# The triangular inverse's levels: products in four array quadrants, a head mask crossed over the partition halves, and weight lows on GpSimd

## The chip, the cores and the metric

One core of a Trainium2 chip runs the whole kernel in one launch. The metric is the device time of one execution in microseconds (us). TensorE multiplies matrices into PSUM; VectorE and ScalarE work elementwise on SBUF and PSUM; GpSimd works elementwise on SBUF alone; SyncE issues the DMAs. Each engine runs its own list of instructions in order, and they wait for one another by semaphores.

## The reference

Two blocks follow one another on 512 tokens of width 1024. The first is an attention and convolution block. The second mixes tokens with twelve recurrent heads of width 64 (an RWKV-7 delta rule) and a small cross attention, and ends with a feed-forward layer. What matters here is the recurrence of the second block:

```
def step(S, inp):
    r_t, w_t, k_t, v_t, a_t, b_t = inp
    sa = jnp.einsum('bhvk,bhk->bhv', S, a_t)
    S = (S * w_t[:, :, None, :] + sa[..., None] * b_t[:, :, None, :]
         + v_t[..., None] * k_t[:, :, None, :])
    return S, jnp.einsum('bhvk,bhk->bhv', S, r_t)
```

The inputs r, k, v come from projections of the normed residual with 1024-row weights; w and a come through low-rank products and sigmoids.

## The kernel before, in words

The recurrence is computed in chunks. The 512 tokens are eight chunks of 64, and inside a chunk the steps become products of 64 by 64 matrices, for which a unit lower triangular matrix of each chunk must be inverted. Two heads are worked on together, a pair; there are six pairs, numbered 0 to 5 (`for p in range(NP)`, on TensorE and on VectorE alike). A tile of 128 partitions holds two chunks at a time, the even one in partitions 0 to 63 and the odd one in 64 to 127 (`PARITIES`, index q), four of these double chunks (`G`, index c) and two heads (index h) side by side. `rows(0)` is the first 64 partitions, `rows(1)` the others.

**The inverse.** Its blocks are doubled level by level: `LEVELS` is 2, 4, 8, 16, 32. In each level b, for each head, TensorE multiplies the strict triangle NT with the inverse so far, XN (`times_inverse`, L1310). VectorE masks the result to the level's band and writes it to Y (L2606). TensorE multiplies Y with XT in both orders (`inverse_update`, L1323 and L1326; in the last level only one, L1336). VectorE adds that to XT and XN (L2641). The next level's product waits for head h's add, separately for each head. Operands and results of one such matmul are 64 partitions high, so each uses a quadrant of the 128x128 array. The stationary and moving operands of `times_inverse` lie in the half 1-q, the output in the half q: of the array's four quadrants, this product uses the two crossed ones. A head's product is eight matmuls, each two instructions in fp32.

**What stands between.** The engines' lists are written out by hand. Between a level's products and its updates, and behind the updates, TensorE has other work: the projection of the next pair's values (half of it in level 4 ahead of the update, the other half behind it), a low-rank gate product in level 8, a sum of squares in level 16, `masked_values` (L1349) behind level 8, sums of a norm (L1237, L1238) behind level 2. In levels 2 to 16 VectorE has the decayed keys and norms of other pairs. At level 8 it starts with `pair_input(p + 1, "v")` (L2067), which waits for ScalarE's part (L1841), then masks, then for p < 5 `unit_key` (L2064) and `bonus_rest` (L2481), then the two adds. Behind the levels come `solve`, the transitions and a chain of six states, beside which the projections of the pair after next run.

**Weights in two parts.** A projection is done as three fp32r matmuls per tile: weights high with data high and low, weights low with data high (L857 to L859). ScalarE rounds a 128x1024 block to its high part (`weights_high`, L1673); VectorE subtracts it from the block to get the low part (`weights_low`, L2123) and raises `w_low`. The product waits for `w_high` and `w_low`; the DMA that refills the block's place waits for `w_low`. The blocks stand in the order of `SPLIT`, and `w_low` counts them. For the pairs' blocks VectorE does this where `weights_after` is called, often several us after the high part is there.

**GpSimd** does four fills and, for pairs 0 and 1, the decayed key KD (L809).

Of the kernel before, what the change touches and what calls it, by code (L numbers as in the profile page):

```python
# [40 lines left out]
F32 = mybir.dt.float32  # L41
F32R = mybir.dt.float32r
ALU = mybir.AluOpType
# [18 lines left out]
C = 64  # L62
NC = S // C
# [19 lines left out]
STEPS = NQ * QT  # L83
MTILES = S // P
MUNITS = 2 * MTILES
MU_AMID, MU_BEHIND = {0: 0, 1: 2, 2: 3, 4: 5}, {0: 1, 3: 4}
MU_SOLVE = len(MU_AMID) + len(MU_BEHIND)
MU_CHAIN = MU_SOLVE + 1
# [331 lines left out]
def build(nc, small, tables, xT, ctxT, memT, weights, saved, outT):  # L420
    plan = psum_plan()
    with ExitStack() as ctx:
# [269 lines left out]
        def group(q):  # L692
            return sum(q >= SPLIT_AT[n] for n in ("out0", "wdad", f"mix{PAIR_MIX}"))
# [21 lines left out]
        def free_inc(ins, name):  # L715
            ins.then_inc(free[plan[name][0]], 1)
# [78 lines left out]
        @block.gpsimd  # L795
        def _(pool):
            pool.memset(QW[:], 0.0).then_inc(filler_ready, 1)
            pool.memset(SILU[:], 0.0).then_inc(zeroed, 1)
            pool.wait_ge(*is_full("ctx_sum"))
            pool.memset(GLU, 0.0).then_inc(zeroed, 1)  # L800
            pool.wait_ge(*is_full("h1_sum"))
            pool.memset(H[:, 0, :], 0.0).then_inc(zeroed, 1)

            for p in range(2):

                pool.wait_ge(bonus_in, p + 1)
                pool.wait_ge(exps_done, p + 1)
                k3, l3 = (x.rearrange("p (c t) -> p c t", c=NC) for x in (QW[:], LG))
                pool.tensor_tensor(KD[p % 2], k3, l3, ALU.mult).then_inc(kd_ready, 1)  # L809


        @block.tensor
        def _(pe):
# [481 lines left out]
            def key_products(name, p, x):  # L1295
                take(name)
                out = by_head(name)
                for c in range(G):
                    for q, h in QH:
                        ins = pe.matmul(out[rows(q), h, c], x[rows(h), 2 * c + q, :],  # L1300
                                        AR[p % 2][rows(h), :, 2 * c + q, :], start=True, stop=True)
                        if c == G - 1:
                            full_inc(ins, name)

            def times_inverse(name, h):

                out = take(name, G * C).rearrange("p (c t) -> p c t", c=G)
                for c in range(G):
                    for q in range(PARITIES):
                        ins = pe.matmul(out[rows(q), c, :], NT[rows(1 - q), h, c, :], XN[rows(1 - q), h, c, :],  # L1310
                                        start=True, stop=True)
                        if c == G - 1:
                            full_inc(ins, name)
# [104 lines left out]
            for p in range(NP):  # L1418
# [14 lines left out]
                for b in LEVELS:  # L1433
                    for h in range(HEADS):
                        if prev is None:
                            pe.wait_ge(x_first, p + 1)
                        else:
                            pe.wait_ge(*is_free(f"x{prev}_{p}_{h}"))
                        times_inverse(f"y{b}_{p}_{h}", h)

                    if p == NP - 1:
                        if b == LEVELS[0]:
                            gn_mean(p - 1)
                        if b == LEVELS[1]:
                            gn_square(p - 1)
                        if b == LEVELS[3]:
                            gate_low_rank(p - 1)
                        memory_unit(MU_AMID.get(LEVELS.index(b)))
                        if b == LEVELS[2]:
                            masked_values(p)  # L1450
                    else:
                        if b == LEVELS[1]:
                            project_part(f"v_{p + 1}", 0, DK // 2)
                        if p and b == LEVELS[2]:
                            gate_low_rank(p - 1)
                        if p and b == LEVELS[3]:
                            gn_square(p - 1)
                        if b == LEVELS[-1] and p + 2 < NP:
                            low_rank(p + 2)
                    for h in range(HEADS):  # L1460

                        pe.wait_ge(*is_free(f"y{b}_{p}_{h}"))
                        if b != LEVELS[-1]:
                            inverse_update(f"x{b}_{p}_{h}", h)
                        else:

                            last_update(f"xf_{p}_{h}", h)
                    if p == NP - 1:
                        memory_unit(MU_BEHIND.get(LEVELS.index(b)))
                    else:  # L1470
                        if p and b == LEVELS[0]:
                            gn_mean(p - 1)
                        if b == LEVELS[1]:
                            project_part(f"v_{p + 1}", DK // 2, DK)
                        if b == LEVELS[2]:
                            masked_values(p)
                        if b == LEVELS[3]:
                            bonus_sum(p + 1)
                        if b == LEVELS[-1]:
                            project_part(beside_chain(p, "k"), 0, 2)  # L1480
                    prev = b
# [572 lines left out]
        def _(vec):  # L2054
# [63 lines left out]
            def weights_low(q):  # L2118

                b = BLOCK_AT[SPLIT[q]]  # L2120
                vec.wait_ge(w_high, q + 1)
                high, low = wsplit(q)
                vec.tensor_tensor(low, room_of(b), high.bitcast(F32), ALU.subtract).then_inc(w_low, 1)  # L2123
# [322 lines left out]
                i = "krv".index(x)  # L2446
                free_inc(shift_end(f"{x}_{p}", 3 + 3 * p + i, MU_PAIR + 3 * p + i, (K0, R0, V0)[i]), f"{x}_{p}")

            def weights_after(p, x):

                if group(SPLIT_AT[f"{x}_{p}"] + 2) == 2:
                    weights_low(SPLIT_AT[f"{x}_{p}"] + 2)

            def chunks(x):
                return x.rearrange("p (c t) -> p c t", c=NC)

# [108 lines left out]
            for p in range(2):  # L2565
                denominator(f"w_{p}")
                denominator(f"A_{p}")
                running_sums(p)
                for x in "kr":
                    pair_input(p, x)  # L2570
                    weights_after(p, x)
                changed_key(p)
                least_norm(p)
                if p == 0:
                    pair_input(0, "v")
                    weights_after(0, "v")
                    bonus(0)
                    decayed_r(0)
                    unit_key(0)
                    decayed_a(0)  # L2580
                    scaled_b(0)
                    decayed_b(0)
                else:
                    decayed_r(1)
            for p in range(NP):
# [14 lines left out]
                for b in LEVELS:  # L2600
                    if p + 1 < NP and b == LEVELS[2]:
                        pair_input(p + 1, "v")
                    for h in range(HEADS):
                        name = f"y{b}_{p}_{h}"
                        vec.wait_ge(*is_full(name))
                        free_inc(vec.tensor_tensor(Y[:, h], bank(name, G * C).rearrange("p (c t) -> p c t", c=G),  # L2606
                                                   mask(f"m{b}", G), ALU.mult), name)

                    if p == NP - 1 and b == LEVELS[0]:
                        gn_centre(p - 1)  # L2610
# [30 lines left out]
                        free_inc(vec.tensor_tensor(old, new, old, ALU.add), name)  # L2641
                    if late and b == LEVELS[1]:
                        decayed_r(late)
                        weights_after(late, "r")
                    if norm_late(p - 1):
                        if b == LEVELS[0]:
                            gn_centre(p - 1)
# [14 lines left out]
                    return x.rearrange("p (c q) t -> p q c t", q=PARITIES)  # L2662

                if p + 1 < NP:
                    weights_after(p + 1, "v")
                    if norm_late(p - 1):
                        gn_finish(p - 1)
                        gate(p - 1)
                    if late:
                        decayed_key(late)  # L2670
                else:
                    for m in range(PAIR_MIX):
                        weights_low(SPLIT_AT[f"mix{m}"])
                    memory_unit(MU_SOLVE)
# [10 lines left out]
                for n in CHAIN:  # L2685
                    name = f"h_{p}_{n}"
                    if p == NP - 1 and n in MU_STEPS:
                        memory_unit(MU_CHAIN + n - 1)
                    vec.wait_ge(*is_full(name))
                    free_inc(scaled_sum(H[:, n + 1, :], bank(name, C), ELC[p % 2][:, n:n + 1], FB[:, n, :]), name)  # L2690
                    if p == NP - 2 and n == G:
                        memory_queries(0)
                    if p == NP - 1 and n in MIXED_AT:
                        if n == min(MIXED_AT):
                            vec.wait_ge(*is_full(f"yu_{p}"))
                        for k in MIXED_AT[n]:
                            mixed_low(k)
                    if p + 2 < NP:
                        if n == 1:
                            denominator(f"w_{p + 2}")  # L2700
                        if n == 2:
                            denominator(f"A_{p + 2}")
                        if n == 3:
                            running_sums(p + 2)
                        if n == 4:
                            pair_input(p + 2, "k")
                        if n == 5:
                            weights_after(p + 2, "k")
                            key_squares_rest(p + 2)
                if p + 2 < NP:  # L2710
                    pair_input(p + 2, "r")
# [214 lines left out]
```

## Time and profile before

| | us |
|---|---|
| median of 3 runs (1069.06 to 1071.4) | 1069.5 |
| the profiled execution | 1070.18 |
| its span | 1068.4 |
| TensorE matmul busy | 1039.6 (97%) |
| VectorE busy | 653.9 (61%) |
| ScalarE busy | 453.0 (42%) |
| GpSimd busy | 5.6 (1%) |
| granted TensorE clock, as a share of full speed | 1.0 |

Busy shares are over the whole span. The levels of the six pairs stand between 386 and 653 us. The ends of matmuls are modelled, so neighbours overlap by some 0.07 us in the list; the distance from start to start is what one costs.

### The profile page before, as it was taken

What the parts mean: (1) busy time and instruction counts of PE and PEld (TensorE: products, weight loads), DVE (VectorE), ACT (ScalarE), POOL (GpSimd) and SP (SyncE); (2) the same over time, 40 slices, a digit from 0 to 9 for tenths busy, and PEclk for the clock granted to TensorE, in tenths of its full rate; (3) what the DMA queues carried; (4) which work ended last, traced back from release to release, by engine and by line L of the source; (5) the groups of instructions that cost most, each with busy time, mean ns of one, the idle gap of its engine ahead of it and who ended that gap; (6) DMA issues with size and microseconds to landing.
All of it is one profiled execution on the core that took longest, in us unless ns stands there. A gap on an engine that the chain in (4) does not pass through costs nothing.

```text
span 1068.4 us, 22579 instructions
## 1 busy us (share of the span) xinstructions
PE 1039.6 (97%) x9816; PEld 823.4 (77%) x9816; DVE 653.9 (61%) x1025; ACT 453.0 (42%) x732; POOL 5.6 (1%) x10
## 2 busy tenths in 40 slices
PE   7999999999999989999999999999999999999998
PEld 5777777676777777777777767787888888888887
DVE  4569999977466665868677667664443223444322
ACT  5455555686335533443535245344432112443111
POOL 0000000000000000000000000000000000000000
PEclk9999999999999999999999999999999999999999
DMA  9912224000532110110110121322222232223230
GB/s 360 377 61 99 79 81 176 1 2 2 197 118 79 60 42 22 43 42 25 39 42 22 42 81 43 124 93 99 99 99 99 99 99 88 93 96 114 89 104 30
DMA packets 26161, 95.01 MB, mean 89 GB/s; under 512 B 2896, under 2 KB 3152, under 8 KB 25552
## 3 DMA queue, kind: packets, MB, share of 16 engines
q1 hardware_dynamic: 26064, 93.57, 25.1%
q8 instruction: 79, 1.29, 0.5%
q14 instruction: 18, 0.15, 0.0%
HBM read 89.36 MB, written 4.19 MB: 88 GB/s over the span
## 4 chain that ended last, share of the span: by engine, by line
PE 76%; DVE 16%; ACT 4%; issue 2%; DMA 1%; SPq 1%; POOL 0%; ACTq 0%; DVEq 0%
PE psum L857 19%; PE psum L858 18%; PE psum L859 18%; DVE work L2067 5%; PE psum L867 3%; PE psum L1310 2%; PE psum L1323 2%; DVE small_temps L2218 1%; PE psum L1045 1%; PE psum L1024 1%; PE psum L1359 1%; PE psum L1382 1%; DMA work<-weights 1%; DVE in_weights_low L2123 1%; PE psum L1110 1%
## 5 line engine op out<-in xcount | busy, mean ns | idle before, releaser
L2123 DVE TENSOR_TENSOR weights_low<-ring,weights_high 128x1024 fp32r<-128x1024 f32 x70 | 85.8, 1226 | 75.3 <-ACT weights_high L1673 75.3
L1673 ACT ACTIVATE weights_high<-ring 128x1024 fp32r<-128x1024 f32 x70 | 73.6, 1052 | 127.5 <-PE psum L859 127.5
L857 PE MATMUL psum<-normed_high,weights_high 128*128 128x512 f32 x256 | 100.2, 391 | 0.2 <-DVE weights_low L2123 0.2
L859 PE MATMUL psum<-normed_high,weights_low 128*128 128x512 f32 x256 | 99.7, 389 | 0.0
L859 PE MATMUL psum<-hidden_high,weights_low 128*128 128x512 f32 x256 | 99.7, 389 | 0.0
L858 PE MATMUL psum<-normed_low,weights_high 128*128 128x512 f32 x256 | 99.6, 389 | 0.0
L858 PE MATMUL psum<-hidden_low,weights_high 128*128 128x512 f32 x256 | 99.6, 389 | 0.0
L857 PE MATMUL psum<-hidden_high,weights_high 128*128 128x512 f32 x256 | 99.6, 389 | 0.0
L2067 DVE SCALAR_TENSOR_TENSOR work<-work,small_sb 128x512 f32<-128x512 f32 x116 | 80.2, 745 | 0.2
L1643 ACT ACTIVATE work<-psum 128x384 f32<-128x384 f32 (+1 forms) x110 | 54.1, 541 | 56.3 <-PE psum L1359 18.8
L857 PE MATMUL psum<-pair_normed_high,pair_weights_high 128*128 128x512 f32 x176 | 75.8, 431 | 0.8 <-DVE normed_low L2127 0.8
L858 PE MATMUL psum<-normed_low,pair_weights_high 128*128 128x512 f32 x176 | 69.3, 394 | 0.0
L859 PE MATMUL psum<-pair_normed_high,pair_weights_low 128*128 128x512 f32 x176 | 68.9, 392 | 0.0
L2046 ACT ACTIVATE work<-work 128x512 f32<-128x512 f32 x32 | 20.2, 632 | 100.9 <-DVE work L2064 100.9
L857 PE MATMUL psum<-normed_high,in_weights_high 128*128 128x512 f32 x144 | 59.2, 411 | 1.9 <-DVE in_weights_low L2123 1.6
L857 PEld LDWEIGHTS psum<-normed_high,weights_high 128*128 128x128 f32 x256 | 48.1, 188 | 10.8 <-issue 0.9
L859 PE MATMUL psum<-normed_high,in_weights_low 128*128 128x512 f32 x144 | 56.2, 390 | 0.0
L858 PE MATMUL psum<-normed_low,in_weights_high 128*128 128x512 f32 x144 | 56.2, 390 | 0.0
L859 PEld LDWEIGHTS psum<-normed_high,weights_low 128*128 128x128 f32 x256 | 48.1, 188 | 10.1
L858 PEld LDWEIGHTS psum<-normed_low,weights_high 128*128 128x128 f32 x256 | 48.1, 188 | 10.1 <-issue 0.2
L859 PEld LDWEIGHTS psum<-hidden_high,weights_low 128*128 128x128 f32 x256 | 48.1, 188 | 10.0
L857 PEld LDWEIGHTS psum<-hidden_high,weights_high 128*128 128x128 f32 x256 | 48.1, 188 | 9.9
(320 smaller groups left out, 2102.6 us busy)
## 6 DMA issues: line engine op xcount, KB each, us to landing
ring<-weights SPq DMA_DIRECT2D x135, 512.0 KB, 3.7
work<-weights SPq DMA_DIRECT2D x10, 512.0 KB, 12.9
residual<-xT SPq DMA_DIRECT2D x4, 512.0 KB, 7.1
mixed<-weights SPq DMA_DIRECT2D x4, 512.0 KB, 7.8
residual_saved<-residual SPq DMA_DIRECT2D x8, 256.0 KB, 4.4
residual<-residual_saved SPq DMA_DIRECT2D x1, 2048.0 KB, 9.0
outT<-residual SPq DMA_DIRECT2D x8, 256.0 KB, 3.3
tables_sb<-tables SPq DMA_DIRECT2D x1, 1280.0 KB, 10.4
```

Of the source, the lines that this page charges most:

```text
L857: pe.matmul(out, wh, high(k), start=first and n == 0, stop=False)
L858: pe.matmul(out, wh, low(k), start=False, stop=False)
L859: ins = pe.matmul(out, wl, high(k), start=False, stop=last and n == len(order) - 1)
L867: full_inc(pe.matmul(take(name, w), stationary, moving, start=True, stop=True), name)
L1024: last = pe.transpose(out[:, t * P:(t + 1) * P], src[:, t * P:(t + 1) * P], tab("ident"))
L1310: ins = pe.matmul(out[rows(q), c, :], NT[rows(1 - q), h, c, :], XN[rows(1 - q), h, c, :], start=True, stop=True)
L1323: ins = pe.matmul(out[rows(q), 0, c, :], Y[rows(q), h, c, :], XT[rows(q), h, c, :], start=True, stop=True)
L1643: free_inc(act.activation(out, bank(name, w) if src is None else src, ACT.Copy), name)
L1673: act.activation(wsplit(q)[0], room_of(b), ACT.Copy).then_inc(w_high, 1)
L2046: act.activation(FS[:, t, :], FS[:, t, :], ACT.Square).then_inc(h_relu, 1)
L2067: return vec.scalar_tensor_tensor(out=out, in0=a, scalar=scalar, in1=b, op0=op, op1=ALU.add)
L2123: vec.tensor_tensor(low, room_of(b), high.bitcast(F32), ALU.subtract).then_inc(w_low, 1)
```

## The change

`times_inverse_both` takes the place of `times_inverse` in levels 4, 8, 16 and 32 (`CROSSED`); level 2 keeps the old form. It issues both heads' matmuls interleaved. Head 0's output goes to the half q as before, head 1's to the half `q ^ 1`, the same as its operands' half, so all four quadrants are used in turn. Both heads' tiles are full at the end, and both heads' adds of the level before are waited for at the start. Head 1's result then lies with its halves exchanged, and VectorE masks it in two instructions of 64 partitions, each reading one half and writing the other.

The lows of the 18 blocks from v_0 to qm1 go from VectorE to GpSimd, with KD of pair 0 behind v_0's and KD of pair 1 behind r_1's; `weights_after` is gone.

```diff
+CROSSED = (4, 8, 16, 32)
 ...
-            for p in range(2):
-
-                pool.wait_ge(bonus_in, p + 1)
-                pool.wait_ge(exps_done, p + 1)
-                k3, l3 = (x.rearrange("p (c t) -> p c t", c=NC) for x in (QW[:], LG))
-                pool.tensor_tensor(KD[p % 2], k3, l3, ALU.mult).then_inc(kd_ready, 1)
+            def weights_low(q):
+                b = BLOCK_AT[SPLIT[q]]
+                pool.wait_ge(w_high, q + 1)
+                high, low = wsplit(q)
+                pool.tensor_tensor(low, room_of(b), high.bitcast(F32), ALU.subtract).then_inc(w_low, 1)
+            first = SPLIT_AT["v_0"]
+            pool.wait_ge(w_low, first)
+            for q in range(first, SPLIT_AT["mix0"]):
+                weights_low(q)
+                if SPLIT[q] in ("v_0", "r_1"):
+                    p = 0 if q == first else 1
+                    pool.wait_ge(bonus_in, p + 1)
+                    pool.wait_ge(exps_done, p + 1)
+                    k3, l3 = (x.rearrange("p (c t) -> p c t", c=NC) for x in (QW[:], LG))
+                    pool.tensor_tensor(KD[p], k3, l3, ALU.mult).then_inc(kd_ready, 1)
 ...
+            def times_inverse_both(p, b):
+                names = [f"y{b}_{p}_{h}" for h in range(HEADS)]
+                outs = [take(name, G * C).rearrange("p (c t) -> p c t", c=G) for name in names]
+                for c in range(G):
+                    for q in range(PARITIES):
+                        for h in range(HEADS):
+                            ins = pe.matmul(outs[h][rows(q ^ h), c, :], NT[rows(1 - q), h, c, :],
+                                            XN[rows(1 - q), h, c, :], start=True, stop=True)
+                            if c == G - 1:
+                                full_inc(ins, names[h])
 ...
-                        times_inverse(f"y{b}_{p}_{h}", h)
+                        if b not in CROSSED:
+                            times_inverse(f"y{b}_{p}_{h}", h)
+                    if b in CROSSED:
+                        times_inverse_both(p, b)
 ...
-                        free_inc(vec.tensor_tensor(Y[:, h], bank(name, G * C).rearrange("p (c t) -> p c t", c=G),
-                                                   mask(f"m{b}", G), ALU.mult), name)
+                        y, m = bank(name, G * C).rearrange("p (c t) -> p c t", c=G), mask(f"m{b}", G)
+                        if h == 0 or b not in CROSSED:
+                            ins = vec.tensor_tensor(Y[:, h], y, m, ALU.mult)
+                        else:
+                            for half in range(2):
+                                ins = vec.tensor_tensor(Y[rows(half), h], y[rows(1 - half)], m[rows(1 - half)], ALU.mult)
+                        free_inc(ins, name)
 ...
                 else:
+                    vec.wait_ge(w_low, SPLIT_AT["mix0"])
                     for m in range(PAIR_MIX):
                         weights_low(SPLIT_AT[f"mix{m}"])
```

## Rows read from the trace of the kernel before

**Rows 1.** The page, busy time, share of the span and instructions of each engine

```profile
PE 1039.6 (97%) x9816; PEld 823.4 (77%) x9816; DVE 653.9 (61%) x1025; ACT 453.0 (42%) x732; POOL 5.6 (1%) x10
```

**Rows 2.** VectorE's line L2123 by tile (ns, min/median/max), and waits of TensorE, 386 to 670

```profile
L2123 DVE TENSOR_TENSOR pair_weights_low<-ring,pair_weights_high x24: 1214/1218/1226, 320.0 to 654.3; 128x1024 fp32r<-128x1024 f32 x24
...
PE psum L1323 <- DVE work L2606: 1.5, 4, 0.9
```

**Rows 3.** Groups of TensorE, 480 to 760 us: busy us, mean ns of one

```profile
L1310 PE MATMUL psum<-work 64*64 64x64 f32 x640 | 23.2, 221 | 0.7 <-DVE work L2641 0.5 <-issue 0.2
...
L1382 PE MATMUL psum<-work 64*64 64x64 f32 x512 | 8.3, 219 | 0.0
```

**Rows 4.** Timeline of TensorE: start us, us, instruction, idle before

```profile
389.30 1.15 PE L1310 MATMUL psum<-work 64*64 64x64 f32 x32 [0.16 <-DVE work L2641]
...
485.54 1.15 PE L1310 MATMUL psum<-work 64*64 64x64 f32 x32
...
493.61 1.15 PE L1310 MATMUL psum<-work 64*64 64x64 f32 x32
494.69 0.70 PE L867 MATMUL psum<-work,small_sb 128*128 128x512 f32 x1
...
497.67 1.15 PE L1310 MATMUL psum<-work 64*64 64x64 f32 x32
...
501.17 1.15 PE L1310 MATMUL psum<-work 64*64 64x64 f32 x32
...
503.45 1.15 PE L1336 MATMUL psum<-work 64*64 64x64 f32 x32
504.53 0.50 PE L857 MATMUL psum<-pair_normed_high,pair_weights_high 128*128 128x512 f32 x1
...
598.45 1.15 PE L1336 MATMUL psum<-work 64*64 64x64 f32 x32 [0.42 <-DVE work L2606]
```

**Rows 5.** Timeline of VectorE, pair 0 and pair 2

```profile
388.73 0.96 DVE L2641 TENSOR_TENSOR work<-psum,work 128x256 f32<-128x256 f32 x2 [0.43 <-PE psum L1326]
...
484.53 0.95 DVE L2641 TENSOR_TENSOR work<-psum,work 128x256 f32<-128x256 f32 x2 [0.43 <-PE psum L1326]
...
494.52 0.75 DVE L2067 SCALAR_TENSOR_TENSOR work<-psum,small_sb,work 128x511 f32<-128x511 f32 x1 [1.41 <-ACT work L1841]
495.18 0.74 DVE L2606 TENSOR_TENSOR work<-psum,tables_sb 128x256 f32<-128x256 f32 x2
495.85 0.74 DVE L2064 SCALAR_TENSOR_TENSOR work<-work,small_sb,head_rstd 128x512 f32<-128x512 f32 x1
496.50 0.69 DVE L2481 TENSOR_TENSOR bonus_low<-t_t,bonus_high 128x512 fp32r<-128x512 f32 x1
497.11 0.75 DVE L2641 TENSOR_TENSOR work<-psum,work 128x256 f32<-128x256 f32 x2
...
502.26 0.75 DVE L2606 TENSOR_TENSOR work<-psum,tables_sb 128x256 f32<-128x256 f32 x2
```

**Rows 6.** Timeline of ScalarE, level 8 of pair 2

```profile
494.38 1.05 ACT L1673 ACTIVATE pair_weights_high<-ring 128x1024 fp32r<-128x1024 f32 x1
```

**Rows 7.** Timeline of VectorE, instructions over 64 partitions

```profile
336.65 0.41 DVE L2074 TENSOR_SCALAR sigmoids<-sigmoids 64x512 f32<-64x512 f32 x1
337.10 0.42 DVE L2415 COPY work<-t_t 64x512 f32<-64x512 f32 x1
```

**Rows 8.** Timelines of GpSimd and VectorE around 381 us, and the same copy at 491

```profile
381.61 1.28 POOL L809 TENSOR_TENSOR work<-weighted,work 128x512 f32<-128x512 f32 x1 [21.15 <-DVE t_t L2064]
...
381.44 0.69 DVE L2485 TENSOR_SCALAR head_rstd<-psum 128x512 f32<-128x512 f32 x1
382.05 0.87 DVE L2497 COPY small_temps<-work 128x8 f32<-128x8 f32 x1
...
491.21 0.16 DVE L2497 COPY small_temps<-work 128x8 f32<-128x8 f32 x1
```

**Rows 9.** Timeline of VectorE, head of pair 0

```profile
385.34 1.22 DVE L2593 TENSOR_TENSOR work<-work,tables_sb 128x1024 f32<-128x1024 f32 x1
```

More of the change, by code:

```diff
@@ L2447, in pair_input @@
                 free_inc(shift_end(f"{x}_{p}", 3 + 3 * p + i, MU_PAIR + 3 * p + i, (K0, R0, V0)[i]), f"{x}_{p}")
-            def weights_after(p, x):
-                if group(SPLIT_AT[f"{x}_{p}"] + 2) == 2:
-                    weights_low(SPLIT_AT[f"{x}_{p}"] + 2)
             def chunks(x):
@@ L2570, in _ @@
                     pair_input(p, x)
-                    weights_after(p, x)
                 changed_key(p)
@@ L2575, in _ @@
                     pair_input(0, "v")
-                    weights_after(0, "v")
                     bonus(0)
@@ L2643, in _ @@
                         decayed_r(late)
-                        weights_after(late, "r")
                     if norm_late(p - 1):
@@ L2664, in _ @@
                 if p + 1 < NP:
-                    weights_after(p + 1, "v")
                     if norm_late(p - 1):
@@ L2707, in _ @@
                         if n == 5:
-                            weights_after(p + 2, "k")
                             key_squares_rest(p + 2)
```

## The prediction, made before the result was known

> **What bounds the kernel now.** I read the page's busy shares first. TensorE is busy for 97% of the span [rows 1]: a microsecond of it left empty is a microsecond of time. VectorE and GpSimd are far below that, so moving work between them pays only where TensorE waits for VectorE. The view of who waited for whom, from 386 to 670 us, has as its largest sum 1.5 us, TensorE on the masks [rows 2]. So the 18 weight lows taken off VectorE (1.22 us each [rows 2]) have little to give back, and the extra work has little room.
>
> Then the order of time. The changed code stands in six pairs of heads, some 48 us each, and I followed pair 2 [rows 4, 5]. Below, "+t" counts from the start of the level's product with NT. The reader is to see in rows 4 that TensorE goes from group to group without a hole, and in rows 5 that in level 8 VectorE does so too, from the values' input to the adds.
>
> **The product in four quadrants.** A level's product is 32 instructions (each matmul is two in fp32). In two quadrants the next group comes 1.08 us after its start (493.61 to 494.69, [rows 4]). By the sums, 640 such instructions take 23.2 us, 36 ns each, while 512 of a product that goes round all four quadrants take 8.3 us, 16 ns [rows 3]. At 16 to 18 ns the 32 take 0.6 us. So 0.48 us per level, 24 levels, 11.5 us, is the most this part can return, and only where nothing else comes last.
>
> **What it adds on VectorE.** Head 1's mask becomes two instructions over 64 partitions. Half the partitions is not half the time: a tensor_scalar over 64x512 took 0.41 us and a copy of 64x512 0.42 us [rows 7]. The copy also shows a second cost. It reads and writes the other half of the partitions than its predecessor, has no wait, and starts 0.04 us after that one's end, where neighbours overlap by 0.08 (334 to 339 against 495.18 to 497.77, [rows 5, 7]). The two half masks change halves each, and so does what follows them. So I take 0.46 us from start to start for these three, where masks without a wait are 0.33 apart. What follows comes later by 0.33 us if nothing is held and by 3 x 0.46 - 2 x 0.33 = 0.71 us if all three are; I take the latter, by the row of the copy. The Trainium skill (VectorE: DVE Perf Modes, section on two Vector instructions with no wait between them) says that an instruction whose input or output starts in another quadrant than the last one's is held until the earlier ones have finished. The trace agrees, with the 0.04 us.
>
> It also ties the heads together: a product of levels 4 to 32 now needs both adds of the level before, where head 0's needed only the first, and head 1's update needs the second half mask. Level 2 itself is unchanged.
>
> **Level 4** (between product and update stand 12 matmuls of a projection). Level 2's adds end at 485.48, and the product started at 485.54 anyway [rows 4, 5]. The masks are hidden, and the adds, behind VectorE at 491.21 [rows 8], are needed at 493.61: -0.48 us, all of it. Pair 0 started level 4 on the first add (389.30, while the second ended at 389.69 [rows 4, 5]): +0.44 takes that back.
>
> **Level 8 is where the change meets itself.** VectorE comes here with the values' input at +0.91, which hangs on ScalarE's part and that on the projection, not on the product. Then mask, mask, unit key, bonus low, add, add, without a hole, and level 16 starts at 497.67, +4.06 [rows 4, 5]. The shorter product gains nothing: TensorE would be through the gate product at +1.65, but mask 0 starts at +1.57 and ends at +2.0. The second half mask ends at +2.92, and what follows is 0.71 late; the adds start at +4.2 and +4.55, the second ends at +4.97 and level 16, which now waits for it, starts at +5.0 if nothing else happens: +0.95.
>
> Now GpSimd. ScalarE's weights high ends at 495.43 [rows 6], +1.82. VectorE made the low long after, at a quiet place; GpSimd starts it at once, about +1.9. How long it takes no row shows: its product over 128x512 took 1.28 us [rows 8], so 128x1024 is between 2.3 (if it grows as VectorE's does, from 0.69 to 1.22 us, [rows 2, 5]) and 2.56 us (twice). I take 2.4, up to +4.3. The unit key (L2064), all of whose tensors lie in SBUF, wants to start at +2.95. What happens to such an instruction? The one place where GpSimd and VectorE overlap is 381.61 to 382.89. VectorE's L2485, reading PSUM, ran its usual 0.69 us. The copy L2497, SBUF to SBUF, lasted 0.87 us against 0.16 elsewhere, and ended with GpSimd's instruction [rows 8]. I take it that the unit key is stopped the same way until +4.3. Then 0.65 to the bonus low, 0.61 to the adds, 0.33 and 0.42 for these: +6.3. Level 16 starts at +6.35, so +2.3 us. Masks and adds read one operand from PSUM and run on. The Trainium skill (SBUF — State Buffer, section on the two sides of SBUF) says that VectorE and GpSimd share a port pair as an exclusive lock, for a VectorE instruction in a two-port mode or with two SBUF inputs, and that the loser waits out the whole instruction. It supports the step from copy to two-input product, which the trace does not show.
>
> This holds for the five pairs that have the values' projection at level 8 (pairs 0 to 4). Elsewhere GpSimd's low starts behind ScalarE's high beside instructions that read PSUM, or has 2.8 us of these in front of it: nil.
>
> **Level 16.** One sum stands between product and update. Mask 0 can start at +0.77, the half masks at +1.23 and +1.69, the last ends at +2.12; head 1's update then runs from +2.17 to +2.87, its add ends at +3.5 behind the decayed a, and level 32 starts at +3.56, against +3.50 (497.67, 501.17, [rows 4]). +0.06. Pair 0 has no sum of squares there, its update waited for the mask alone, and by the same chain it loses 0.5.
>
> **Level 32.** A low-rank product stands in between (pairs 0 to 3). After the second add VectorE has two instructions of 0.6 us, then mask 0 at +1.06, halves at +1.52 and +1.98, the last ends at +2.41. TensorE is through at +1.81 (2.28 before, 501.17 to 503.45 [rows 4]) and does head 0's update, 0.54 us; head 1's starts at +2.46, and the next projection at +3.0 instead of +3.36 (504.53, [rows 4]): -0.32. Pair 4 has nothing in between and already waited for its mask, 0.42 us (598.45, [rows 4]); the last half mask comes 0.35 late there: +0.35.
>
> **Sum.** Pairs 1 to 3: -0.48 + 2.3 + 0.06 - 0.32 = 1.56 us, 4.7 in all. Pair 4: 2.2. Pair 0: -0.04 + 2.3 + 0.5 - 0.32 = 2.4. Pair 5 has no GpSimd work; its waits for both adds and longer mask chains against shorter products: +0.2, an estimate. Before the first pair: the first low is on TensorE's way at its start, +0.15. And the pair's head: the lows of v_1 and k_2 (GpSimd's queue holds them behind the second decayed key) now fall on 382 to 387, where VectorE has the copy, L2500, three masks from PSUM and L2593, whose two inputs are both in SBUF and which releases level 2 [rows 8, 9]. VectorE comes there up to 1.2 us earlier without its own low, GpSimd's two times 2.4 us then stop L2500 and L2593 in turn. L2593 starts about 387.5 instead of 385.34: +2.2 (bounds -0.7 and +3.9, if GpSimd loses or wins every contest). Together 4.7 + 2.2 + 2.4 + 0.2 + 0.15 + 2.2 = 11.9 us. The profiled execution took 1070.2 us (span 1068.4), so 1082.1; the median of three was 0.7 less: 1081.
>
> SP's loads wait for the lows. Those of r_1 to r_2 come 1 to 6 us later, at least 3 us ahead of their use; later ones come earlier. Nil.
>
> **Rivals.**
> 1. Only SBUF copies are stopped, not products with two inputs. Then level 8 costs 0.95: pairs 1 to 3 0.2 each, pair 4 0.9, pair 0 1.1, pair 5 0.2, the head -0.7, 0.15. Sum +2.3: 1072. For it: the only stopped instruction seen is a copy.
> 2. GpSimd is slower than twice its 128x512, or wins each contest: 3.4 us instead of 2.4 adds 1 us in five levels, 0.5 at L2593 in the pairs' heads, and takes the 3.9: about +20, 1089. For it: the page calls GpSimd's spans rough.
> 3. The other side, faster: TensorE's product is what counts. Nothing stops the unit key and nothing holds the halves, which start 0.33 apart. Level 4 gives 0.48, level 16 0.3, level 32 0.48; level 8 still costs 0.6 for one mask more and the second add. That is -0.65 in pairs 1 to 3, about +0.1 in pairs 0 and 4 together, -0.3 in pair 5, and -0.7 in the head: -2.9 + 0.15, 1067. It decides if, in level 8, the second add ends by +4.6. Against it: rows 7 and 8. If moreover a half mask cost half, level 8 would be as before and the time 1064.
>
> **Chances.** Forecast 0.63 (own range 1078 to 1085, from 2.3 to 2.56 us for a low and the head's bounds), rival 1 0.18, rival 2 0.06, rival 3 0.13. A measurement tells 0.2%, 2.1 us, from no change: faster 0.1 (most of rival 3), within 0.13 (the rest of it and half of rival 1), slower 0.77. The range 1068 to 1087 takes in rival 1 and leaves out rival 2 and most of rival 3.
>
> **What would show it.** GpSimd with 18 instructions of 128x1024, near 2.4 us (much above 3: rival 2). L2064 in level 8 lasting about 2 us or starting late, and ending with GpSimd's: the stop; 0.75 us beside a running GpSimd: rival 1. Half masks 0.46 apart or 0.33. TensorE without work for some 2 us ahead of level 16's product in five pairs. Level 4's product followed after 0.6 us by the projection; if after 1.08, the four quadrants do not run together and the part gives nothing (+4 us on the sum). The whole argument is wrong if level 16 still starts near +4.1.

## The result, and the profile after

The changed kernel takes 1082.37 us (median of 4 runs, 1081.04 to 1084.09) where the kernel before takes 1069.28 beside it: ratio 1.0115, 95% interval 1.0093 to 1.0138. It is slower, by 13.1 us. The profiled execution took 1084.09 us, span 1082.3, which is 13.9 more than the span before.

The page after, busy time, share of the span and instructions of each engine:

```profile
span 1082.3 us, 22605 instructions
PE 1039.7 (96%) x9816; PEld 818.8 (76%) x9816; DVE 653.0 (60%) x1031; ACT 453.0 (42%) x732; POOL 50.4 (5%) x28
```

Against [rows 1], TensorE did the same number of instructions in the same busy time, and its idle time grew from 28.8 to 42.6 us. The equal busy time is a balance of two things: in the kernel of the first experiment, with the new product and masks alone, it is 1034.3 us, 5.3 less, and the changed kernel spends 13.7 us at the lower clock, where its instructions last longer. GpSimd has 18 instructions more and 45 us. VectorE lost the 18 lows (22 us) and yet is busy for only 0.9 us less. 24 masks became 48 halves of the same length (+10 us, at 0.42 each); the other 11 us are instructions that now last longer.

The waits of TensorE from 386 to 684 us (us in total, times, longest):

```profile
PE psum L1324 <- DVE work L2666: 9.6, 8, 1.5
PE psum L1347 <- DVE work L2628: 3.6, 9, 1.4
PE psum L1347 <- DVE work L2631: 2.4, 9, 0.3
```

L1324 is the product in four quadrants, L2666 the adds of the level before. Before, the largest sum of this view was 1.5 us [rows 2]; now TensorE waits 9.6 us for the adds, 7.6 of them in five waits at the end of level 8. Level 8 is the place. Timelines of pair 1, first TensorE, then VectorE, then GpSimd (start us, us, instruction, idle before):

```profile
449.54 0.69 PE L1324 MATMUL psum<-work 64*64 64x64 f32 x32
450.16 1.13 PE L879 MATMUL psum<-work,small_sb 128*128 128x512 f32 x2
...
455.71 0.69 PE L1324 MATMUL psum<-work 64*64 64x64 f32 x32 [1.52 <-DVE work L2666]
```

```profile
450.45 0.75 DVE L2094 SCALAR_TENSOR_TENSOR work<-psum,small_sb,work 128x511 f32<-128x511 f32 x1 [1.81 <-ACT work L1868]
451.12 0.41 DVE L2628 TENSOR_TENSOR work<-psum,tables_sb 128x256 f32<-128x256 f32 x1
451.56 0.86 DVE L2631 TENSOR_TENSOR work<-psum,tables_sb 64x256 f32<-64x256 f32 x2
452.45 1.89 DVE L2091 SCALAR_TENSOR_TENSOR work<-work,small_sb,head_rstd 128x512 f32<-128x512 f32 x1
454.26 0.68 DVE L2503 TENSOR_TENSOR bonus_low<-t_t,bonus_high 128x512 fp32r<-128x512 f32 x1
454.87 0.74 DVE L2666 TENSOR_TENSOR work<-psum,work 128x256 f32<-128x256 f32 x2
```

```profile
451.44 2.35 POOL L810 TENSOR_TENSOR pair_weights_low<-ring,pair_weights_high 128x1024 fp32r<-128x1024 f32 x1 [14.59 <-ACT pair_weights_high L1700]
```

The product's follower comes 0.62 us after its start (1.08 before, [rows 4]): the quadrants do run together. But the unit key (L2091), 0.74 us in [rows 5], lasts 1.89 us and ends 0.55 us after GpSimd's low (453.79). The adds end behind it, and level 16 starts at +6.17 where it started at +4.06. TensorE stands 1.52 us right before that product, in pairs 0 to 4 alike. The half masks (L2631) run wholly beside the same low; they read one operand from PSUM, write to SBUF, and keep their 0.43 and 0.42 us.

Level by level, start to start, in us (before / after), read from the starts of the level's product:

| pair | level 2 | level 4 | level 8 | level 16 | level 32 to next pair |
|---|---|---|---|---|---|
| 0 | 2.65 / 3.13 | 8.10 / 8.51 | 4.06 / 6.16 | 3.05 / 4.44 | 28.84 / 30.12 |
| 1 | 3.09 / 3.16 | 8.07 / 7.61 | 4.07 / 6.17 | 3.50 / 4.44 | 30.38 / 29.68 |
| 2 | 3.08 / 3.20 | 8.06 / 7.61 | 4.06 / 6.17 | 3.50 / 4.44 | 28.89 / 28.63 |
| 3 | 3.09 / 3.17 | 8.07 / 7.69 | 4.06 / 6.17 | 3.93 / 3.57 | 28.96 / 28.80 |
| 4 | 3.09 / 3.17 | 8.06 / 7.65 | 4.07 / 6.17 | 3.50 / 3.57 | 30.11 / 30.46 |
| 5 | 5.74 / 5.74 | 4.95 / 4.92 | 5.36 / 6.08 | 5.78 / 5.84 | |

The first product of the first pair starts 0.26 us earlier than before (386.40 against 386.66), so nothing was lost up to there.

Level 16 has two lengths, and the reason stands in the granted clock. Stretches of the kernel after (columns: us, then busy us of TensorE, weight loads, VectorE, ScalarE, GpSimd with counts, granted clock, DMA share, GB/s): the first in level 16 of pair 1, the second of pair 2, the third in levels 16 and 32 of pair 0, the last in level 16 of pair 3:

```profile
457.10:460.50 3.40, 3.40 (x78) 2.58 (x82) 2.90 (x7) 1.23 (x2) 0.00 (x0) 0.51 0.02 5
508.30:511.70 3.40, 3.40 (x82) 2.51 (x80) 2.87 (x7) 1.14 (x2) 0.00 (x0) 0.51 0.00 0
405.90:412.70 6.80, 6.58 (x107) 4.03 (x98) 5.08 (x10) 0.89 (x2) 0.00 (x0) 0.50 0.00 0
558.00:561.00 3.00, 2.75 (x100) 2.00 (x98) 2.92 (x8) 1.23 (x2) 0.00 (x0) 1.00 0.03 10
```

The clock is at the lower of its two levels, 1.2 GHz, in three of five pairs, beginning 1.4 to 1.7 us after TensorE resumed work in level 16. In the profiled execution before the change it was at the upper one, 2.4 GHz, all through the recurrences. Pair 3's level 16, 3.93 before the change, holds a stall inside its product (0.23 us, during which TensorE waits for nothing that the profile shows), so its 3.57 is no gain of the change.

### The profile page after: what moved, and what is told of

The parts are those of the page before. It is cut to its first block, busy times and chain, and to the rows that moved or that the text cites. A ratio compares the mean times of both kernels' runs of the same rounds, so it can differ in the third digit from the quotient of the medians.

```text
span 1082.3 us, 22605 instructions
## 1 busy us (share of the span) xinstructions
PE 1039.7 (96%) x9816; PEld 818.8 (76%) x9816; DVE 653.0 (60%) x1031; ACT 453.0 (42%) x732; POOL 50.4 (5%) x28
## 4 chain that ended last, share of the span: by engine, by line
PE 72%; DVE 19%; ACT 4%; issue 2%; DMA 1%; SPq 1%; POOL 0%; ACTq 0%; DVEq 0%
PE psum L869 19%; PE psum L870 18%; PE psum L871 18%; DVE work L2094 6%; PE psum L879 2%; DVE small_temps L2245 2%; DVE work L2091 1%; DMA ring<-weights 1%; PE psum L1347 1%; PE psum L1057 1%; PE psum L1324 1%; PE psum L1036 1%; PE psum L1383 1%; PE psum L1406 1%; DVE work L2631 1%
```

## The experiments

**The two halves of the change apart, and the lows moved or cut.** Four kernels. Products alone: the four-quadrant product and the crossed masks, with the lows on VectorE.

> The change's products and crossed masks alone; all lows on VectorE as before. Theory (GpSimd's product stops VectorE's instructions that have all tensors in SBUF, and holds the unit key of level 8): level 8 takes 5.0 us from its product to level 16's instead of 6.17, level 4 7.6, and the time is 1069.3 + about 3 = 1072. Rival A (the crossed masks and the wait for both adds are the cost, GpSimd's lows nearly free): level 8 still near 6 us, 1080 or more.

Lows alone: GpSimd makes them, products and masks as before.

> GpSimd's lows alone; products and masks as before. Theory: in level 8 the unit key is still stopped, for it could start at +2.24 and GpSimd holds it to about +4.3, so the level takes 5.9 us instead of 4.06, in five pairs, less 0.5 at the first pair's head: 1069.3 + 9 = 1078, more if TensorE's clock falls as it did in the change's profile. Rival A: near 1069.

Lows late: the changed kernel, but the one low that falls on level 8 waits for the pair's last add.

```diff
+            late = {SPLIT_AT["qm1" if p + 2 == NP else f"r_{p + 2}"]: p for p in range(NP - 1)}
             for q in range(first, SPLIT_AT["mix0"]):
+                if q in late:
+                    pool.wait_ge(*is_free(f"xf_{late[q]}_1"))
                 weights_low(q)
```

> The whole change, but the five lows that fell on level 8 (r_2 to r_5 and qm1) wait on GpSimd for the second add of level 32, the place where VectorE made them. Theory: the unit key lasts 0.75 us again, level 8 takes 5.0 us, no granted clock under 1.0 in the pairs, and the time is some 0.5 us under the products-only kernel: 1071.5. Rival A: 1082 as the change. Rival B (it is GpSimd's work as such that slows VectorE or TensorE, wherever it stands): 1082 too, with the cost moved.

Lows in four: each low as four instructions over 256 columns.

```diff
-                pool.tensor_tensor(low, room_of(b), high.bitcast(F32), ALU.subtract).then_inc(w_low, 1)
+                n = D // 4
+                for i in range(4):
+                    at = slice(i * n, (i + 1) * n)
+                    ins = pool.tensor_tensor(low[:, at], room_of(b)[:, at], high.bitcast(F32)[:, at], ALU.subtract)
+                ins.then_inc(w_low, 1)
```

> The whole change, each GpSimd low cut into four products of 128x256. Theory (an exclusive hold for one instruction): a piece lasts about 0.75 us, the unit key gets in after the piece that is running, near +3.4, and ends near +4.0 instead of +4.8; the bonus low may meet the next piece. Level 8 takes 5.3 to 5.9 us, the time is 1077 to 1080. Rival C (the two engines share the port and both go slower): the unit key ends as late as in the change, 1082.

Measured, beside the kernel before at 1069.80:

| kernel | us | ratio, 95% | level 8 | level 16 | TensorE idle before level 16 |
|---|---|---|---|---|---|
| products alone | 1073.37 | 1.0040 (1.0026 to 1.0053) | 5.03 | 3.57 | 0.38 |
| lows alone | 1080.48 | 1.0100 (1.0076 to 1.0123) | 5.89 | 3.49 (pair 0: 3.05) | 1.67 to 1.75 |
| lows late | 1075.45 | 1.0057 (1.0037 to 1.0076) | 5.03 | 3.57 | 0.38 |
| lows in four | 1079.67 | 1.0097 (1.0076 to 1.0118) | 5.76 | 3.57 (pair 0: 4.44) | 1.11 |

Each half is slower than the kernel before, and the lows are the larger one. VectorE and GpSimd in level 8 of pair 2, in the products alone (first fence), the lows alone (second and third), the lows in four (fourth and fifth), and GpSimd and VectorE with the lows late (last):

```profile
495.50 0.41 DVE L2624 TENSOR_TENSOR work<-psum,tables_sb 128x256 f32<-128x256 f32 x1
495.95 0.86 DVE L2627 TENSOR_TENSOR work<-psum,tables_sb 64x256 f32<-64x256 f32 x2
496.84 0.75 DVE L2080 SCALAR_TENSOR_TENSOR work<-work,small_sb,head_rstd 128x512 f32<-128x512 f32 x1
```

```profile
499.06 0.74 DVE L2628 TENSOR_TENSOR work<-psum,tables_sb 128x256 f32<-128x256 f32 x2
499.72 2.57 DVE L2091 SCALAR_TENSOR_TENSOR work<-work,small_sb,head_rstd 128x512 f32<-128x512 f32 x1
```

```profile
499.38 2.36 POOL L810 TENSOR_TENSOR pair_weights_low<-ring,pair_weights_high 128x1024 fp32r<-128x1024 f32 x1 [16.50 <-ACT pair_weights_high L1700]
```

```profile
499.50 0.95 DVE L2095 SCALAR_TENSOR_TENSOR work<-work,small_sb,head_rstd 128x512 f32<-128x512 f32 x1
500.37 1.21 DVE L2507 TENSOR_TENSOR bonus_low<-t_t,bonus_high 128x512 fp32r<-128x512 f32 x1
```

```profile
498.48 3.68 POOL L813 TENSOR_TENSOR pair_weights_low<-ring,pair_weights_high 128x256 fp32r<-128x256 f32 x4 [15.27 <-ACT pair_weights_high L1704]
```

```profile
507.32 2.80 POOL L810 TENSOR_TENSOR pair_weights_low<-ring,pair_weights_high 128x1024 fp32r<-128x1024 f32 x1 [25.15 <-DVE work L2669]
...
507.94 2.73 DVE L2097 SCALAR_TENSOR_TENSOR mixed<-mixed,small_sb,tables_sb 128x512 f32<-128x512 f32 x1
```

Without a running low the unit key lasts 0.75 us, with one 2.57, with the pieces 0.95. In the lows alone it starts 0.7 us earlier after the level's start than in the changed kernel and ends at the same +4.8, 0.55 us behind GpSimd: the end of the low sets it, not its own start. So the two halves don't add in level 8 (0.97 and 1.83 alone, 2.10 together): the crossed masks cost only 0.28 where the stop covers them. Cut in four, the stops are short, but two VectorE instructions in a row now meet them, GpSimd takes 3.68 us for what took 2.36, and level 8 gives back 0.4 us. Moved away from level 8, the low meets another product of two SBUF operands (L2097), which lasts 2.73 us in place of 0.75, and is itself stretched to 2.80. No wait of TensorE grows by that, and level 8 is exactly that of the products alone. So a stop costs time only where TensorE waits for what is stopped.

Two expectations missed. The lows alone were expected at 1078 and took 1080.5: level 8 was as expected, but TensorE loses another 1.0 us inside pair 0's level 4, most of it with "issue" as its end (time in which it waits for nothing that the profile shows), and 1.6 us behind the recurrences, where this execution has a stretch of 3.4 us at the lower clock (at 678 us) and the profiled one before has none. The late lows were expected 0.5 us under the products alone and took 2.1 more; of the 1.7 us between the two profiled spans, 1.5 are longer "issue" waits of TensorE (2.2 in all against 0.7). What causes them is not shown.

**A hold, or the price of 64 partitions?** The kernel before with head 1's mask in two halves that do not cross.

```diff
+                            for half in range(2):
+                                ins = vec.tensor_tensor(Y[rows(half), h], y[rows(half)], m[rows(half)], ALU.mult)
```

> The kernel before, with head 1's mask in levels 4 to 32 made by two instructions over 64 partitions each, not crossed: input and output lie in the same half. Products, lows and adds are as before. Theory (an instruction is held until the one before has ended where its input or output begins in another half): the first half mask is not held and starts 0.33 us behind head 0's; the second and what follows it are held, 0.44 us apart. Level 8 gets 0.5 us longer by it (4.06 to about 4.6), some 3 us in all. Rival: an instruction over 64 partitions costs 0.44 from start to start wherever it lies: the first half mask starts 0.33 us behind a full mask in either case, the second 0.44 after, the follower 0.44 after; told apart by the first half mask, which in the changed kernel started 0.03 us behind the end of its predecessor. Rival: no hold without crossing: all 0.33 apart, level 8 4.4.

1075.12 us, ratio 1.0051 (1.0035 to 1.0067); level 8 takes 4.74 to 4.75. VectorE in level 8 of pair 2:

```profile
496.48 0.42 DVE L2608 TENSOR_TENSOR work<-psum,tables_sb 128x256 f32<-128x256 f32 x1
496.81 0.85 DVE L2611 TENSOR_TENSOR work<-psum,tables_sb 64x256 f32<-64x256 f32 x2
497.69 0.75 DVE L2064 SCALAR_TENSOR_TENSOR work<-work,small_sb,head_rstd 128x512 f32<-128x512 f32 x1
```

The first half, in the same partitions as its predecessor, starts 0.33 us after it, 0.09 before that one's end. The second, in the other half, starts 0.42 after the first (0.01 behind its end), and the unit key 0.46 after that (0.03 behind the end). In the products alone all three started behind the end (0.44 to 0.46 apart). It is the change of halves that holds, not the size. That is the rule of the Trainium skill named in the prediction (VectorE: DVE Perf Modes, section on two Vector instructions with no wait between them), and here the trace agrees for masks that read PSUM. The straight halves cost level 8 0.68 us where the crossed ones cost 0.97; the difference also holds the wait for the second add and the shorter product. The time went up by more than the levels show (4.0 us up to level 32 of pair 5, 5.6 in the span). The other 1.6 us come behind the recurrences, where this execution has a stretch of 3.4 us at the lower clock (at 673 us).

**Only where it pays.** The products and masks in level 4 alone (`if b in CROSSED`, with `CROSSED = (4,)`), lows on VectorE:

> The kernel before with the four-quadrant product and the crossed masks in level 4 alone; the weight lows stay on VectorE. Theory: level 4 is the one level where a later reader takes up the masks, so its step falls from 8.06 to 7.6 us (as in the run with the products alone), levels 8, 16 and 32 keep 4.06, 3.50 and their length, and level 2 pays 0.07 us (pair 0: 0.48) for the second add: 5 pairs at -0.37, pair 0 nil, together -1.5 us, 1068.0 to 1068.5 against 1069.8. Rival: the shorter level 4 brings level 8 no sooner than VectorE allows, and level 8 grows by what level 4 gave: no change. Rival: the stalls of TensorE that end with no wait (instruction supply, 0.6 to 1.2 us here and there) move about and hide it.

The same with level 32 of pairs 0 to 3:

> As the run with level 4 alone, and the same product also in level 32 of pairs 0 to 3. In the run with the products alone level 32 was 2.20 us from its start to the last update, where 2.28 stood before and 1.81 was forecast: the second half of the low-rank gate product waits for VectorE's read of the bonus sums' bank. Theory: by that the step gives 0.08 us a pair, 0.3 in all: about 1068.0. Rival (the forecast's): 0.32 a pair, 1067.0.

And that with VectorE's read of the bonus sums moved up:

```diff
                     if p + 1 < NP and b == LEVELS[3]:
-                        scaled_b(p + 1)
                         bonus(p + 1)
+                        scaled_b(p + 1)
```

> As the run with levels 4 and 32, and VectorE reads the bonus sums from PSUM before it makes the scaled b, where it did so after it: the bank comes free 0.5 us earlier. Theory: the second half of the low-rank product then starts 0.15 us behind the first as before the change, the last update starts at +1.8 after level 32's start in place of +2.2, the half masks are last (+2.4), and the next projection starts at +3.0 in place of +3.28: 0.25 us a pair in four pairs, about 1067. Rival: the bonus sums are not there yet and VectorE waits 0.2 us or more, which moves the masks and takes it back: as the run before it. If the second half still starts 0.53 us behind, the bank is not what it waits for.

| kernel | us (12 runs) | ratio to 1068.94 (30 runs), 95% |
|---|---|---|
| level 4 | 1067.31 | 0.9984 (0.9975 to 0.9994) |
| levels 4 and 32 | 1067.38 | 0.9979 (0.9971 to 0.9988) |
| and the bonus first | 1067.69 | 0.9983 (0.9975 to 0.9992) |

All three beat both kernels, by 1.3 to 1.6 us by the medians, and can't be told from each other. TensorE in level 4 of pair 2, in the kernel with level 4 alone: level 4's product, its follower, and level 8's product in the old form.

```profile
484.33 0.69 PE L1313 MATMUL psum<-work 64*64 64x64 f32 x32
484.95 0.50 PE L858 MATMUL psum<-pair_normed_high,pair_weights_high 128*128 128x512 f32 x1
...
491.98 1.15 PE L1323 MATMUL psum<-work 64*64 64x64 f32 x32
```

7.65 us for the level against 8.07 [rows 4], with levels 8 and 16 unchanged at 4.06 and 3.49. Level 4 of pair 5 gives as much, 4.50 for 4.95, where the full change gave 0.03: level 8's product in the old form stands 0.25 us there for head 0's add, the new one 0.67 for both. The step of level 32 is told from the changed kernel, pair 3, first TensorE, then VectorE:

```profile
560.48 0.70 PE L1324 MATMUL psum<-work 64*64 64x64 f32 x32
561.10 1.65 PE L879 MATMUL psum<-work,small_sb 64*128 64x512 f32 x4
562.68 1.15 PE L1360 MATMUL psum<-work 64*64 64x64 f32 x32
563.76 0.50 PE L869 MATMUL psum<-pair_normed_high,pair_weights_high 128*128 128x512 f32 x1
```

```profile
560.89 0.68 DVE L2515 TENSOR_TENSOR tables_sb<-psum,work 128x512 f32<-128x512 f32 x1
```

The product is done after 0.62 us, but the low-rank product behind it now lasts 1.58 us to its follower, where it took 1.2 in pair 2 of the kernel before (to 503.45, [rows 4]):

```profile
502.24 1.28 PE L867 MATMUL psum<-work,small_sb 64*128 64x512 f32 x4
```

In the changed kernel its second half needs the bank that L2515 reads until 561.57, and starts at 561.63. So the next projection comes at +3.28 instead of +3.36: 0.08 us gained, not 0.32. With the bonus read first (VectorE, then TensorE, pair 3):

```profile
546.47 0.69 DVE L2515 TENSOR_TENSOR tables_sb<-psum,work 128x512 f32<-128x512 f32 x1 [0.23 <-PE psum L1245]
```

```profile
546.35 0.69 PE L1319 MATMUL psum<-work 64*64 64x64 f32 x32
546.97 1.37 PE L874 MATMUL psum<-work,small_sb 64*128 64x512 f32 x4
548.27 1.45 PE L1355 MATMUL psum<-work 64*64 64x64 f32 x32
549.65 0.50 PE L864 MATMUL psum<-pair_normed_high,pair_weights_high 128*128 128x512 f32 x1
```

The bank is what it waited for: the low-rank product ends its turn after 1.3 us and the update starts at +1.92. But VectorE waits 0.23 us for the sums, the half masks follow as late, the update's second half waits for them, and the projection stands at +3.30. The expectation's rival held; the gain went into the next wait.

**Lows on GpSimd away from level 8.** Level 4 alone, with the late lows:

> The run with level 4 alone, with the weight lows on GpSimd as in the changed kernel, but the one that fell on level 8 starts only when the pair's last add is done. Theory: the lows cost nothing where they meet no VectorE instruction with two SBUF inputs, so levels 4 to 32 are as with level 4 alone (7.6, 4.06, 3.5 us); what is left is the stall of TensorE inside pair 0's level 4 that every run with GpSimd lows had (0.4 to 1.4 us) and longer such stalls in the chains (+2 us in the run with late lows against the products alone): 1069, no better than level 4 alone at 1067.3. Rival: the lows taken off VectorE give something back in the pairs' heads: 1066.5.

1068.54 us, ratio 0.9994 (0.9985 to 1.0003). Levels 8 and 16 are those of the kernel before. Its waits of TensorE start with this row:

```profile
PE psum L1409 <- issue: 2.5, 2, 1.3
```

and inside pair 0's level 4 it has another such stall. No gain can be told from the lows: 22 us less on VectorE are worth nothing here, as TensorE doesn't wait for it where they stood. They are not free of stops either; the moved ones meet L2097 as in the late lows.

## Why the prediction came out right, and where it did not

The time was forecast at 1081 and is 1082.4, for the reason given: in level 8 GpSimd's low stops the unit key. Term by term, in us, from the profiled executions:

| term | forecast | measured |
|---|---|---|
| before the first product (first low, head of pair 0) | +2.35 | -0.26 |
| levels 2 and 4, pairs 0 to 4 | -1.96 | -0.46 |
| level 8, pairs 0 to 4 | +11.5 | +10.5 |
| level 16, pairs 0 to 4 | +0.74 | +2.98 |
| level 32 to the next pair | -0.93 | +0.51 |
| pair 5 | +0.2 | +0.75 |
| sum | 11.9 | 14.0 (span 13.9) |

- **Level 8** was right in each step: GpSimd starts at +1.90 (forecast +1.9), takes 2.35 us (2.4), stops the unit key, which is taken up again at GpSimd's end. The three held instructions are 0.44 apart (0.46). Level 16 starts at +6.17, not +6.35: the bonus low comes 0.47 us behind GpSimd's end, not 0.65. The forecast's 0.71 for the held masks is 0.72 by its own numbers, which changes nothing. Rival 1, only copies are stopped, fell here, and rival 3 with it. The Trainium skill (SBUF — State Buffer, section on the two sides of SBUF) has a two-input product with SBUF operands among what is stopped; the trace now shows it, with 1.89 and 2.57 us for 0.75.
- **Level 4** gives 0.38 to 0.46 in pairs 1 to 4 (forecast 0.48). "Level 2 itself is unchanged" was wrong by 0.07 to 0.12: level 4's product waits for the second add. In pair 0 the two levels together were forecast at -0.04 and measured +0.89: the product stalls inside itself with "issue" as its end (0.57 us), and its follower comes after 1.48 us instead of 0.62. No such stall was forecast. It is there in each run with lows on GpSimd (0.3 to 0.6 us with the new product, 0.8 without), not in the products alone, and its cause is open.
- **Level 16** at the upper clock takes 3.57 (forecast 3.56), and in pair 0 of the products alone 3.05 became 3.57 (forecast +0.5).
- **Level 32** failed in "TensorE is through at +1.81": it assumed that the low-rank product behind follows at its old length. The bank it needs sets its end at +2.20. (The forecast's own +3.0 against +3.36 gives 0.36, where its sum has 0.32.) I had looked for what the masks wait for, not for what bank the instruction behind the faster one takes. Pair 4's +0.35 was right.
- **Head of pair 0**, +2.2, was the largest error. VectorE and GpSimd there, after:

```profile
382.37 0.68 DVE L2522 TENSOR_TENSOR work<-work 128x512 f32<-128x512 f32 x1
...
384.87 1.47 DVE L2613 TENSOR_TENSOR work<-work,tables_sb 128x1024 f32<-128x1024 f32 x1
```

```profile
382.38 6.19 POOL L810 TENSOR_TENSOR pair_weights_low<-ring,pair_weights_high 128x1024 fp32r<-128x1024 f32 x2
```

The step that failed is "GpSimd's two times 2.4 us then stop L2500 and L2593 in turn". VectorE's product (L2522) started first, by 0.02 us, and the first low took 2.88 us, to 385.27. L2613 was waiting by then and went before the second low, losing 0.25 us (1.47 against 1.22, [rows 9]); the second low took 3.35. The three other runs with whole lows on GpSimd went the same way. GpSimd lost 1.5 us of the contest and VectorE a quarter of one, so the head came out near the lower bound that the prediction gave.
- **What no term had**: the clock. At 1.2 GHz level 16 takes 4.44 in place of 3.57, 0.87 in each of three pairs, and pair 0's level 32 1.3 more than with the products alone; pairs 1 and 2 get 0.2 each back in level 32, where the low-rank product no longer waits for its bank. That is about 3.5 us in this execution. The other executions of the changed kernel had mean clocks of 0.998, 0.995 and 0.996 against 0.993, and the one at 0.998 is the fastest, 1081.04. In the profiled executions of the other kernels, the clock kept its upper level in the recurrences wherever TensorE stood 0.38 us or less before level 16; it fell once in the lows in four (1.11 us). The lows alone stood longest, 1.67, and kept it too, so standing there is not enough; what decides stays open.
- **Pair 5** pays 0.72 in level 8, in the products alone as well: VectorE's part of the memory attention, behind the held masks, releases ScalarE's exponentials, and these release TensorE at +3.34 instead of +3.04, and level 16's product stands 0.66 us for the second add where it stood 0.23 for the first. The estimate had 0.2 for the whole pair.

So the sum was good to 2 us in part by luck. The terms are off by -2.6 (head), +1.5 (levels 2 and 4), -1.0 (level 8), +2.2 (level 16), +1.4 (level 32) and +0.6 (pair 5), and the error in the head met the clock's 3.5, which no term had. The mechanism, its place and its size in level 8 (10.5 of the 14) stand shown.

## What to carry to other kernels

Work moved to an idle GpSimd is not free: where it overlaps a VectorE instruction whose inputs both lie in SBUF, the one that comes second waits until the other has ended. Look for what VectorE does in the 2.4 us after the high's end, and let GpSimd start where TensorE waits for none of it; even so it must give something back, and here nothing was waiting for VectorE where the lows had stood. A matmul group made shorter pays only where the group behind it has its bank and its masks in time: of four levels one did in full, and making only that one faster gave the 0.15% that there was. Splitting a VectorE instruction by partition halves costs about a full instruction more: each change of half takes 0.42 to 0.46 us from start to start, where masks without a wait are 0.33 apart, since it waits for the end of the one before.

## What the runs showed of the hardware

- GpSimd's fp32 subtract over 128x1024 lasts 2.35 to 2.40 us undisturbed and 2.57 to 2.58 in four places where its record starts beside VectorE's L2486, a product of two SBUF operands; VectorE takes 1.22 for it [rows 2].
- A stopped VectorE instruction is shown as lasting longer, not as starting late, and ends 0.55 us after GpSimd's record (453.79 and 454.34; 501.74 and 502.29).
- A queued GpSimd instruction doesn't go ahead of a VectorE instruction that already waits: of two lows back to back, L2613 ran between them, and so it did in all four runs with whole lows on GpSimd.
- The 32 product instructions start 15 ns apart on average in four quadrants (the group behind follows after 0.62 us) and 30 ns apart in two (after 1.08), with the same 0.22 us each.
- TensorE's granted clock can fall 1.4 to 1.7 us after it has resumed from 1.5 us without work, in some pairs and not in others. The stretches at 1.2 GHz were 3.4 us long in two pairs and 6.8 us in one.
